# The start of a hybrid decoder kernel: the order of its first transfers and matmuls, and who shifts and scales the input tiles

## What is computed

```python
cs = silu(c)
mod = cs @ ada_w + ada_b                       # 1024 -> 6144: sh1, sc1, g1, sh2, sc2, g2
h = rms(x, norm_mix) * (1 + sc1) + sh1
x = x + g1 * mixer(h, w_in, ...)               # three causal branches, one input projection
h = rms(x, norm_ffn) * (1 + sc2) + sh2
x = x + g2 * moe(h, ...)                       # 64 experts, top 6, and a shared one
return rms(x, norm_final)
```

## Time and profile before

| | us |
|---|---|
| runs of the kernel before | 1509.74, 1506.16, 1514.27 |
| their median | 1509.74 |
| the profiled execution, its own time | 1510.68 |
| its span in the trace | 1508.9 |
| what lies outside the span | 1.8 |

### The profile page before, as it was taken

One profiled execution on the slowest core, in us unless ns is written; L12 is line 12 of the kernel. 1 busy time (PEld: TensorE's weight loads), 2 busy tenths in 40 slices (PEclk: granted clock), 3 DMA queues, 4 the chain that ended last, 5 costly groups with the idle time before them and its releaser, 6 DMA issues.

```text
span 1508.9 us, 19392 instructions
## 1 busy us (share of the span) xinstructions
PE 1336.3 (89%) x6386; PEld 1022.8 (68%) x6386; DVE 1052.2 (70%) x1292; ACT 783.2 (52%) x957; POOL 435.8 (29%) x323
## 2 busy tenths in 40 slices
PE   3897888897798889998978699999999999999984
PEld 1585778555455446877964588788788888887851
DVE  0438684376499664444448698888888989898928
ACT  3623331333333444222131488888888888887811
POOL 1100010002141000000000366566666666565610
PEclk9999989888899989999989899999999999999997
DMA  9224312101122604324132699999999999999856
GB/s 301 70 84 140 112 30 83 42 15 46 59 70 98 236 2 168 98 86 158 58 126 84 241 377 391 395 386 390 369 346 378 364 351 350 364 362 342 314 221 231
DMA packets 126585, 314.57 MB, mean 208 GB/s; under 512 B 24197, under 2 KB 61386, under 8 KB 118090
## 3 DMA queue, kind: packets, MB, share of 16 engines
q1 hardware_dynamic: 108250, 288.73, 53.0%
q0 software_dynamic: 18288, 25.21, 4.6%
HBM read 316.49 MB, written 38.80 MB: 235 GB/s over the span
## 4 chain that ended last, share of the span: by engine, by line
PE 56%; DVE 16%; DMA 13%; ACT 7%; issue 5%; POOL 2%; SPq 1%; POOLq 0%; DVEq 0%; ACTq 0%
PE bank L868 13%; PE bank L1234 8%; DMA arena<-h_dram,tok_of 8%; PE bank L1262 7%; PE bank L873 6%; PE bank L1238 4%; DMA ring<-in_exp_w_up 3%; PE bank L1221 3%; DVE arena L1959 2%; DVE top L1958 2%; POOL tok_of L767 2%; DMA ring<-in_w_in 1%; PE bank L1167 1%; PE bank L837 1%; PE bank L1111 1%
## 5 line engine op out<-in xcount | busy, mean ns | idle before, releaser
L2203 DVE TENSOR_TENSOR ring_parts<-ring,arena_parts 128x2048 fp32r<-128x2048 f32 x186 | 423.0, 2289 | 58.8 <-ACT arena_parts L1590 57.9
L1590 ACT ACTIVATE arena_parts<-ring 128x2048 fp32r<-128x2048 f32 x186 | 355.7, 1931 | 43.9 <-DMA ring<-in_exp_w_up 42.1
L1234 PE MATMUL bank<-arena_parts,oTA_parts 128*128 128x512 f32 x496 | 199.9, 403 | 2.3 <-DVE oTC_parts L2218 1.5
L1234 PE MATMUL bank<-arena_parts,oTC_parts 128*128 128x512 f32 x496 | 194.5, 392 | 0.0
L1262 PE MATMUL bank<-arena_parts,oTB_parts 128*128 128x512 f32 x496 | 160.9, 406 | 5.1 <-DVE ring_parts L2203 5.1
L868 PE MATMUL bank<-hT_parts,ring_parts 128*128 128x512 f32 x344 | 149.7, 435 | 7.7 <-ACT arena L1513 3.7
L755 POOL DMA_INDIRECT arena<-h_dram,tok_of x63 | 134.4, 2134 | 56.2 <-POOL tok_of L767 52.7
L781 POOL DMA_INDIRECT y_dram<-arena,row_of x62 | 97.8, 1577 | 177.7 <-ACT arena L1617 176.8
L868 PE MATMUL bank<-x_parts,ring_parts 128*128 128x512 f32 x344 | 142.0, 413 | 0.0
L1238 PE MATMUL bank<-ring_parts,oTA_parts 128*128 128x512 f32 x496 | 133.5, 391 | 0.0
L767 POOL COPY tok_of<-toks 128x1 int32 (+1 forms) x63 | 117.8, 1870 | 27.9 <-DVE toks L2195 16.4
(11 more groups left out here) (414 smaller groups left out, 2238.4 us busy)
## 6 DMA issues: line engine op xcount, KB each, us to landing
ring<-in_exp_w_gate SPq DMA_DIRECT2D x124, 512.0 KB, 5.4
ring<-in_exp_w_up SPq DMA_DIRECT2D x124, 512.0 KB, 9.3
ring<-in_exp_w_down SPq DMA_DIRECT2D x62, 1024.0 KB, 9.4
ring<-in_w_in SPq DMA_DIRECT2D x25, 1024.0 KB, 5.4
ring<-in_ada_w SPq DMA_DIRECT2D x16, 1024.0 KB, 5.8
arena<-y_dram SPq DMA_DIRECT2D x8, 1536.0 KB, 9.7
arena<-in_ada_w SPq DMA_DIRECT2D x4, 2048.0 KB, 13.3
x<-in_x SPq DMA_DIRECT2D x2, 2048.0 KB, 9.4
```

The costliest lines, as they stand in the source:

```text
L1234: mm(out_gu, t[c][:, tile_cols(4 * k + j)], hi[:, :, j, :], start=(k == 0 and j == 0 and x_ == 0), stop=False)
L1590: A(w_hi[c][k], w_raw[c][k], ACT.Copy).then_inc(sem("gu_hi_ready" if k < 2 else "down_hi_ready"), 1)
L2203: v.tensor_tensor(w_lo[c][k], w_raw[c][k], w_hi[c][k].bitcast(F32), ALU.subtract).then_inc(sem("gu_lo_ready" if k < 2 else "down_lo_ready" ...
```

## The change

Six edits, all in the first 60 us:

1. SP issues `c` and modulation chunk 0 first, on one semaphore; `x` and the small constants follow, then chunks 1 and 2. After `pa0` it issues chunk 3, after `pa1` the four column groups of `wsm` (now counted on chunk 1's semaphore), and then the ring. `wki` and `rbias` move behind the fourth ring piece.
2. ScalarE computes `cs` as soon as `c` and chunk 0 are there, and copies `pa0` ahead of the sums of squares.
3. TensorE's order is pa0, mc0, pa1, pa2, mc1, params, xT0 to xT4, mc2, pa3, mc3, xT5 to xT7; from the third chunk on a chunk is multiplied before the column sums of the one before it. `xT` banks are freed by `hT_lo_ready`, no longer by `hT_ready`.
4. VectorE scales two of the four `xn` tiles.
5. VectorE makes five of the eight `h32` tiles (0, 2, 3, 5, 7), ScalarE three (1, 4, 6); there are four `h32` buffers.
6. ScalarE rounds `wsm` after the copy of `pa3`, `w_qa` after tile 5, and `w_ka` and `w_va0` after the tiles.

```diff
+ACT_SHIFTS = (1, 4, 6)
...
-    out = [("params", "params_ready", 1)]
-    for c in range(4):
-        out += [(f"pa{c}", "cond_ready", c + 1), (f"mc{c}", "mc_ready", c + 1)]
-    out += [(f"xT{j}", "hT_ready", j + 1) for j in range(8)]
+    pa = [(f"pa{c}", "cond_ready", c + 1) for c in range(4)]
+    mc = [(f"mc{c}", "mc_ready", c + 1) for c in range(4)]
+    xt = [(f"xT{j}", "hT_lo_ready", j + 1) for j in range(8)]
+    out = [pa[0], mc[0], pa[1], pa[2], mc[1], ("params", "params_ready", 1)] + xt[:5] + [mc[2], pa[3], mc[3]] + xt[5:]
...
-        h32 = [r0.take(T) for _ in range(2)]
+        h32 = [r0.take(T) for _ in range(4)]
...
-            const(c_in[:, :], a["c"].rearrange("o (p j) -> (o p) j", j=8))
+            def load_ada(c):
+                sp.dma_start(adaw[c % 3], ada[:, :, 512 * c:512 * c + 512]).then_inc(sem(f"ada_loaded{c % 3}"), 16)
+
+            sp.dma_start(c_in[:, :], a["c"].rearrange("o (p j) -> (o p) j", j=8)).then_inc(sem("ada_loaded0"), 16)
+            load_ada(0)
             sp.dma_start(x[:, :, :], a["x"][0].rearrange("(i p) d -> p i d", p=P)).then_inc(sem("x_loaded"), 16)
...
+            load_ada(1)
+            load_ada(2)
+            done(sp, "pa0")
+            load_ada(3)
+            done(sp, "pa1")
             sp.wait_ge(sem("cleared"), SMALL_CLEARED)
             for name, g in GAPS.items():
-                const(wsm[:, :, g:g + IN_SIZES[name]], w_in[:, :, COL[name]:COL[name] + IN_SIZES[name]])
-            const(wki[:, :, :], w_in[:, :, COL["k_idx"]:COL["k_idx"] + 32])
-            const(rbias[:, :], a["router_bias"].to_broadcast([P, E]))
-            for c in range(4):
-                if c == 3:
-                    done(sp, "pa0")
-                sp.dma_start(adaw[c % 3], ada[:, :, 512 * c:512 * c + 512]).then_inc(sem(f"ada_loaded{c % 3}"), 16)
+                sp.dma_start(wsm[:, :, g:g + IN_SIZES[name]], w_in[:, :, COL[name]:COL[name] + IN_SIZES[name]]
+                             ).then_inc(sem("ada_loaded1"), 16)
...
+                if name == "adr00":
+                    sp.dma_start(wki[:, :, :], w_in[:, :, COL["k_idx"]:COL["k_idx"] + 32]).then_inc(sem("extra_loaded"), 16)
+                    sp.dma_start(rbias[:, :], a["router_bias"].to_broadcast([P, E])).then_inc(sem("extra_loaded"), 16)
...
+            first_condition(0)
+            pe.wait_ge(sem("cleared"), CONSTS_READY)
+            first_sums(0)
+            first_condition(1)
+            first_condition(2)
+            first_sums(1)
+            pe.wait_ge(sem("consts_loaded"), NCONST[0])
+            b = begin("params")
+            end(nc.tensor.transpose(b[:, 0:53], prow[0:53, :], ident[0:53, 0:53]))
+            pe.wait_ge(sem("xn_ready"), TT)
+            for j in range(5):
+                turn_rows(j)
+            first_sums(2)
+            first_condition(3)
+            first_sums(3)
+            for j in range(5, 8):
+                turn_rows(j)
...
+            act.wait_ge(sem("ada_loaded0"), 32)
+            A(cs[:, :], c_in[:, :], ACT.Silu).then_inc(sem("cs_ready"), 1)
...
+            keep_condition("pa0", cond0[0])
             act.wait_ge(sem("x_loaded"), 16)
...
+            keep_condition("pa1", cond0[1])
+            act.wait_ge(sem("rstd_ready"), 1)
+            for i in range(2, TT):
+                A(xn[:, i, :], x[:, i, :], ACT.Copy, scale=stat[:, 8 + i:9 + i]).then_inc(sem("xn_ready"), 1)
+            done(act, "mc0")
+            keep_condition("pa2", cond0[0])
             done(act, "mc1")
             keep_condition("pa3", cond0[1])
-            for name in ("w_ka", "w_va0"):
-                split_hi(name)
+            act.wait_ge(sem("ada_loaded1"), 80)
+            A(wsm_hi, wsm, ACT.Copy).then_inc(sem("few_hi_ready"), 1)
             act.wait_ge(sem("mod1_ready"), 1)
             for j in range(8):
                 b = done(act, f"xT{j}")
-                if j >= 2:
-                    act.wait_ge(sem("hT_lo_ready"), j - 1)
-                A(h32[j % 2], b[:, :], ACT.Identity, scale=mod1[:, j:j + 1], bias=mod1[:, 8 + j:9 + j]
-                  ).then_inc(sem("h32_ready"), 1)
+                if j in ACT_SHIFTS:
+                    if j >= 4:
+                        act.wait_ge(sem("hT_lo_ready"), j - 3)
+                    A(h32[j % 4], b[:, :], ACT.Identity, scale=mod1[:, j:j + 1], bias=mod1[:, 8 + j:9 + j]
+                      ).then_inc(sem("h32_ready"), 1)
                 A(hT_hi[:, j, :], b[:, :], ACT.Identity, scale=mod1[:, j:j + 1], bias=mod1[:, 8 + j:9 + j]
                   ).then_inc(sem("hT_ready"), 1)
+                if j == 5:
+                    split_hi("w_qa")
+            split_hi("w_ka")
+            split_hi("w_va0")
...
+            for i in range(2):
+                v.tensor_scalar(xn[:, i, :], x[:, i, :], stat[:, 8 + i:9 + i], None, ALU.mult).then_inc(sem("xn_ready"), 1)
             b = done(dve, "params")
...
+            def shifted(j):
+                if j in ACT_SHIFTS:
+                    return
+                b = done(dve, f"xT{j}")
+                if j >= 4:
+                    dve.wait_ge(sem("hT_lo_ready"), j - 3)
+                dve.wait_ge(sem("hT_ready"), j + 1)
...
+                v.tensor_scalar(h32[j % 4], b[:, :], mod1[:, j:j + 1], mod1[:, 8 + j:9 + j], ALU.mult, ALU.add
+                                ).then_inc(sem("dve_chain"), 1)
+
+            shifted(0)
+            dve.wait_ge(sem("ada_loaded1"), 80)
             dve.wait_ge(sem("few_hi_ready"), 1)
             v.tensor_tensor(wsm_lo, wsm, wsm_hi.bitcast(F32), ALU.subtract).then_inc(sem("few_lo_ready"), 1)
             for j in range(8):
-                dve.wait_ge(sem("h32_ready"), j + 1)
+                if j < 7:
+                    shifted(j + 1)
...
                 dve.wait_ge(sem("hT_ready"), j + 1)
-                v.tensor_tensor(hT_lo[:, j, :], h32[j % 2], hT_hi[:, j, :].bitcast(F32), ALU.subtract
+                v.tensor_tensor(hT_lo[:, j, :], h32[j % 4], hT_hi[:, j, :].bitcast(F32), ALU.subtract
```

More of the change, by code:

```diff
@@ L816, in end @@
                 ins.then_inc(sem("products_done"), 1)
[L818 to L821, removed]
             def column_sums(name, c, sums):
@@ L847, in further_condition, with turn_rows @@
                 condition(f"pb{c}", halves)
[L849 to L855, removed]
+            def turn_rows(j):
                 b = begin(f"xT{j}")
@@ L859, in _, with first_condition, first_sums @@
                 end(ins)
+            pe.wait_ge(sem("cs_ready"), 1)
+            pe.wait_ge(sem("ada_loaded0"), 32)
+            def first_condition(c):
+                if c:
+                    pe.wait_ge(sem(f"ada_loaded{c % 3}"), (32, 16, 16, 48)[c])
+                condition(f"pa{c}", lambda h: adaw[c % 3][:, 4 * h:4 * h + 4, :])
+            def first_sums(c):
+                column_sums(f"mc{c}", c, cond0[c % 2])
+            first_condition(0)
[15 more added lines that the diff above has]
+                turn_rows(j)
             def triple(out, n, weights, tokens, weights_left=True, name=None):
@@ L1045, in _ @@
             end(ins)
-            pe.wait_ge(sem("extra_loaded"), 64)
+            pe.wait_ge(sem("extra_loaded"), 96)
             b = begin("uk")
@@ L1318, in link, with keep_condition @@
                 act.wait_ge(sem("act_chain"), chain[0])
+            act.wait_ge(sem("ada_loaded0"), 32)
+            A(cs[:, :], c_in[:, :], ACT.Silu).then_inc(sem("cs_ready"), 1)
             act.wait_ge(sem("cleared"), CONSTS_READY)
-            act.wait_ge(sem("consts_loaded"), NCONST[0])
-            A(cs[:, :], c_in[:, :], ACT.Silu).then_inc(sem("cs_ready"), 1)
+            def keep_condition(name, out):
+                b = done(act, name)
+                A(out, b[:, :], ACT.Copy).then_inc(sem("cond_ready"), 1)
+            keep_condition("pa0", cond0[0])
             act.wait_ge(sem("x_loaded"), 16)
@@ L1326, in _ @@
             A(stat[:, 4:8], stat[:, 0:4], ACT.Sqrt, scale=1.0 / D, bias=epsc[:, 0:1]).then_inc(sem("rms_ready"), 1)
-            act.wait_ge(sem("rstd_ready"), 1)
-            def keep_condition(name, out):
-                b = done(act, name)
-                A(out, b[:, :], ACT.Copy).then_inc(sem("cond_ready"), 1)
[L1334 to L1339, removed]
             def split_hi(name):
@@ L1672, in _ @@
             link(v.tensor_scalar(level_mask[:, 6, :], level_mask[:, 6, :], 2.0, None, ALU.is_lt))
-            dve.wait_ge(sem("consts_loaded"), NCONST[0])
+            dve.wait_ge(sem("rms_ready"), 1)
+            v.reciprocal(stat[:, 8:12], stat[:, 4:8]).then_inc(sem("rstd_ready"), 1)
+            dve.wait_ge(sem("rstd_ready"), 1)
+            dve.wait_ge(sem("x_loaded"), 16)
+            for i in range(2):
+                v.tensor_scalar(xn[:, i, :], x[:, i, :], stat[:, 8 + i:9 + i], None, ALU.mult).then_inc(sem("xn_ready"), 1)
             b = done(dve, "params")
@@ L1699, in _ @@
                                    op1=ALU.mult).then_inc(sem("mod1_ready"), 1)
+            dve.wait_ge(sem("mod1_ready"), 1)
```

(21 more changed lines are left out.)

10 lines of the change are left out of this document (3 added, 7 removed).

## The result

The changed kernel takes 1498.09 us (median of six runs, 1496.85 to 1499.83) against 1509.62 us for the kernel before (six runs): a ratio of 0.9921, 95% interval 0.9903 to 0.9939, 11.5 us faster. Two later comparisons of the unedited kernel gave 0.9902 (0.9878 to 0.9927) and 0.9905 (0.9881 to 0.9928). The forecast was 1503.7 us, 1498.7 to 1508.2: right in direction, about half of the gain, and the median is just outside the range.

What follows compares the result with a forecast made beforehand. TensorE and ScalarE were taken to bound the chunk rounds at the start, behind a late start. The gain, 3.7 us to mod1, 4.8 through the tiles, 6.0 through `small`, gave 1503.7 us, range 1498.7 to 1508.2.

Steps and rivals of the forecast that it cites:

- The bound of today: Start up to qa0 (68.28 us): TensorE and ScalarE bound the chunk rounds behind a late start; the gain is a shift.
- step 1: First chunk: chunk 0, issued at 1.4, lands at 9.8 (9.5 to 10.8); pa0 10 us earlier, not itself the gain.
- Step 2: Stretch to mod1: the queue bounds it, TensorE at low-level prices; mod1 at 44.9 instead of 48.6, gain 3.7 us.
- Rival A: Clock rises early, before pa3: pa3 1.9 instead of 3.6, 2.5 us more, gain 8.5, 1501.2 us; chance 0.28.
- Step 3: The tiles: VectorE becomes the bound with 10.5 us; last low part at 56.6 instead of 61.4, gain 4.8 us.
- Step 4: The `small` matmuls: start at the low level, end at 59.6 (58.9 to 62.8) instead of 65.6, gain 6.0 us.
- Step 5: From `small` on: copy, la and qa0 keep their distances and everything later shifts with them; sum 6.0 us.
- The covers: Start: work costed at nothing because ready in time: row norm (4.7 us of cover), chunk 3, wsm, ring pieces.
- The bound of 5.4 us for the small transfers: SP's queue: wsm's short rows, wki and rbias take at most 5.4 us, drawn from the old queue.
- Rival D: Slower: ScalarE waits for a late wsm transfer before the first tile; 1518 us, chance 0.04.
- B's dearer chunk 0: Rival on VectorE or queue: chunk 0 lands at 10.8, a shift costs 0.9; gain 3.5, 1506.2 us, chance 0.15.
- The rule and the row: TensorE's transposes: the skill says they don't engage the full clock; the trace showed them falling from 421 to 272 ns.

Runs made afterwards that it cites:

- u_first: Changed kernel with chunk 0 issued behind x and the small constants instead of first; ratio to the kernel before 0.9927.
- a_third: Changed kernel again, no edit, profiled once more; one time, 1508.4 us.
- b_third: Kernel before, no edit, a third profile of it; one time, 1511.2 us.
- w_before: Kernel before with ten extra matmuls on TensorE, results not used, while it waits for the constants; ratio to the kernel before 1.0005.
- u_small: Changed kernel with the wsm column groups, wki and rbias issued ahead of chunks 1 to 3 again; ratio to the kernel before 0.9984.
- r_after: Changed kernel again, no edit, compared beside the others; ratio to the kernel before 0.9902.
- u_dve: Changed kernel with all eight h32 tiles on ScalarE again; ratio to the kernel before 0.9950.
- u_round: Changed kernel with ScalarE's roundings of w_qa, w_ka and w_va0 ahead of the tiles again; ratio to the kernel before 0.9980.
- d_qa: Changed kernel with ScalarE's rounding of w_qa behind tile 7 instead of tile 5; ratio to the kernel before 0.9933.

## Why the prediction was wrong

**The bound of today and step 1.** Right that the gain is a shift made before `qa0`. Chunk 0 took 10.6 us from its issue, not 8.4, beyond the dearer end (9.4); all later landings are 1.8 to 2.2 us late by that, at the spacing of 5.4 that was forecast. x, issued right behind it, was there at about 17.5. Why the pair took longer than either alone is open. `pa0` still started at 12.3, only 0.9 late: ScalarE's table load, 1.28 us on the forecast's chain, was over at 2.1, long before the chunk was there. As step 1 said, the early chunk is not the gain (u_first).

**Step 2 failed, at its first assumption,** that low-level prices hold for all that the change moves forward. a_third, whose clock was low, bears that out: `mod1` at 44.8 and `qa0` at 62.2, where the working had 44.9 and 62.2. That both are met to 0.1 is partly luck (the late chunk 2 and partly high `pa2`, `mc2` and `mc3` cancel). In the other four profiles the clock was high, and the terms measured: `pa3` 1.9 for 3.6, `mc1`, `mc2` and `mc3` 1.0 each for 1.87, five `xT` 2.3 for 4.2, and in three of the four `pa2` 1.9 for 3.6. `mod1` was at 38.2 to 40.1, 5 to 7 us earlier than forecast. In the first profile this closes the sum: with chunk 2 at 28.5 the working would give 47.1, these terms take off 6.5 (there `pa2` only 0.3, at 3.33), and the 40.6 left compares with 40.3 measured. `mod1` came 4.8 us before its forecast and `qa0` 5.0, so the other steps hardly missed. Rival A named the mechanism with 0.28 and priced it 2.5 us; it left out the sums and `pa2`. Seven profiles of eight had `pa3` high, so it deserved the larger chance.

**Not seen at all: what the clock is worth depends on the order of ScalarE's work.** The earlier trace rows had the roundings on the chain at 46.30, and the prediction read them as 1.1 us of delay. They were a wall at the landing of the third ring piece (46.2 in b_third, 47.5 in w_before, and 1.9 us of rounding behind it), and with it the old kernel gains 1.4 us from a fast clock (b_third), the new one up to 7.

**Step 3 was right in kind:** VectorE bounds the tiles, 11.8 us to the last low part against 11.7 forecast, with the one wait of 1.0 (forecast 0.4) for the tile behind `w_qa`. A shift on VectorE costs 0.80 to 0.81 us, not 0.75, and two subtractions in a row 1.28, not 1.38.

**Step 4.** From the last low part at 51.9 to the end of `small` at 54.6: 2.7 us, forecast 3.0. **Step 5** held: 1440.0 against 1440.7 from `qa0` to the end. That it held to 0.7 is partly luck: five profiles of the changed kernel lie between 1435.4 and 1444.4 there.

**The covers held** for x's norm, chunk 3, `wsm` and the ring. The bound of 5.4 us for the small transfers was wrong for a fuller queue (7.3 in u_small), without harm where the change put them. Rival D did not happen; B's dearer chunk 0 did, and was overtaken by A.

**The rule and the row.** The prediction held against the Trainium skill, TensorE: Matmul & The Clock Gate, Part 4: PE-mode transpose, that the clock rose among transposes. The runs leave it undecided what transposes do to the rise. In the changed kernel's profile and in r_after the level was already high when the transposes began, so something else raised it: chunk matmuls. In a_third 20 transposes inside an unbroken run stayed low for 4.5 us, and in u_small again, which is on the rule's side. In u_dve, u_round and d_qa, as in the kernel before, the rise fell inside the transposes: theirs start at 421 ns and end at 273. And where the level was high already, as in r_after, all twenty ran at 272 to 328 ns, so they do run at the high level. What decides the moment is not settled here.

## What to carry to other kernels

Before pricing a stretch near the start, find TensorE's level from the durations of one form in two places, and then ask of both kernels what they can do with the other level; a gain that exists only at one of them needs its own sum. When a chain is shortened, look at every instruction that an engine has queued ahead of the chain's next link: one that stood level with the old bound becomes the new one. And transfers of very short rows belong behind the large ones that something waits for, not between them (7.3 us here).

## What was unexpected in the hardware

- The granted clock in the records is listed as 1.00 for the whole start of the kernel before, while chunk matmuls took 1061 ns and the same ones later 592. The level at the start is to be read from durations. A window over `mc2` and most of `pa3`, all at low-level prices, lists the clock the same way (PE, PEld, DVE, ACT, POOL busy, clock, DMA share, GB/s):

```profile
40.00:45.00 5.00, 4.86 (x24) 2.37 (x24) 0.16 (x1) 2.83 (x3) 0.00 (x0) 1.00 1.09 343
```

- The moment of the rise differs between executions of the same program: `pa2` took 3.33, 1.92, 3.06, 1.93 and 1.92 us in five profiles of the changed kernel, and `qa0` lay between 55.2 and 62.2. Executions of one program differed by 15 us (1493.0 to 1508.4).
- A column sum against a vector of ones is not cheap for its one moving column: eight recorded matmuls took 1.87 us low, 0.23 each, as much as each of the sixteen with 512 columns of a chunk, and 0.98 to 1.05 high. Their weight loads fill that time; in the kernel before, the load rows of `mc0`:

```profile
27.77 1.78 PEld L827 LDWEIGHTS bank<-groups,arena 128*128 128x128 f32 x8 [4.37 <-ACT arena L1332]
```


- Four transfers of 128 KB in all, in rows of 16 to 64 bytes, took SP 11.1 us to issue, and together with `wki` and `rbias` they put the large chunks behind them back by 7.3 us.
